# A two-block transformer kernel: two expert weight units loaded beside the ring, the context product moved behind the first expert quad

## What is computed

```python
x = x + g1 * (mix @ w_out[l])
h2 = rms_norm(x, norm2_w[l]) * (1 + sc2) + sh2
x = x + g2 * hier_moe(h2, w_group[l], b_group[l], w_expert[l], b_expert[l], w1[l], w3[l], w2[l])
...
xcn = modulate(rms_norm_2(hc, norm_mix_g[layer]), csh1, csc1)   # hc: the 256 context tokens
kv_c = xcn @ w_in[:, Q_END:]                                    # the context product
```

## Time and profile before

| what | value |
|---|---|
| median of 3 runs | 1784.64 us (1783.9 to 1785.4) |
| profiled execution, its own time | 1785.08 us |
| its span in the trace | 1783.3 us |
| PE / DVE / ACT busy | 78% / 34% / 11% |
| DMA mean | 331 GB/s |
| chain that ended last | DMA 49%, PE 43%, DVE 6% |

### The profile page before, as it was taken

One profiled execution on the slowest core, in us unless ns is written; L12 is line 12 of the kernel. 1 busy time (PEld: TensorE's weight loads), 2 busy tenths in 40 slices (PEclk: granted clock), 3 DMA queues, 4 the chain that ended last, 5 costly groups with the idle time before them and its releaser, 6 DMA issues.

```text
span 1783.3 us, 24407 instructions
## 1 busy us (share of the span) xinstructions
PE 1390.6 (78%) x10622; PEld 864.8 (48%) x10623; DVE 612.4 (34%) x968; ACT 197.6 (11%) x440; POOL 5.0 (0%) x10
## 2 busy tenths in 40 slices
PE   6798996666666756765766666667998999989997
PEld 4796863222122212221222122215876999879997
DVE  2367637000000000000000000017445777767775
ACT  2003321000000000000000000001422000120001
POOL 1000000000000000000000000000000000000000
PEclk8988998888788788788888789878998999989999
DMA  9979955999999999999999999995943555414541
GB/s 401 356 316 423 378 203 246 429 429 428 429 429 429 429 428 429 429 428 429 429 429 429 428 429 429 428 427 205 405 178 138 186 206 187 166 52 173 211 167 69
DMA packets 46263, 590.03 MB, mean 331 GB/s; under 512 B 5328, under 2 KB 7792, under 8 KB 9088
## 3 DMA queue, kind: packets, MB, share of 16 engines
q1 hardware_dynamic: 42464, 581.86, 79.0%
q10 hardware_dynamic: 3744, 7.37, 1.2%
HBM read 586.58 MB, written 2.62 MB: 330 GB/s over the span
## 4 chain that ended last, share of the span: by engine, by line
DMA 49%; PE 43%; DVE 6%; issue 1%; ACT 1%; SPq 0%; DVEq 0%; ACTq 0%
DMA ring<-in_w 44%; PE ps L1874 5%; PE ps L1875 5%; PE ps L1879 5%; PE ps L1441 3%; PE ps L1706 3%; PE ps L1613 3%; PE ps L1385 3%; PE ps L1721 2%; PE ps L1893 2%; PE ps L1892 2%; PE ps L1890 2%; DMA ring<-in_w_in 2%; DMA ring<-in_w_ada 1%; DVE ring_parts L750 1%
## 5 line engine op out<-in xcount | busy, mean ns | idle before, releaser
L1706 PE MATMUL ps<-ring,mixT 128*32 128x512 f32 x2048 | 307.1, 734 | 182.4 <-DMA ring<-in_w 180.9
L1721 PE MATMUL ps<-ring,arena 128*32 128x512 f32 x1024 | 175.3, 820 | 107.2 <-DMA ring<-in_w 96.0
L1706 PEld LDWEIGHTS ps<-ring,mixT 128*32 128x32 f32 x2048 | 62.0, 121 | 401.0 <-DMA ring<-in_w 278.0
L750 DVE TENSOR_TENSOR ring_parts<-ring,ring_parts 128x1024 fp32r<-128x1024 f32 (+3 forms) x119 | 189.7, 1625 | 1.0
L1112 DVE TENSOR_TENSOR arena<-arena,ps 128x512 f32<-128x512 f32 x16 | 11.0, 688 | 511.4 <-PE ps L1706 511.3
L1874 PE MATMUL ps<-mixT_parts,ring_parts 128*128 128x256 f32 x704 | 173.3, 283 | 6.7 <-issue 6.7
L1875 PE MATMUL ps<-mixT_parts,ring_parts 128*128 128x256 f32 x704 | 172.8, 283 | 0.0
L1721 PEld LDWEIGHTS ps<-ring,arena 128*32 128x32 f32 x1024 | 33.0, 131 | 232.8 <-DMA ring<-in_w 149.1
L747 DVE CAST ring_parts<-ring 128x1024 fp32r<-128x1024 f32 (+3 forms) x119 | 100.4, 890 | 132.4 <-DMA ring<-in_f 75.0
L1874 PEld LDWEIGHTS ps<-mixT_parts,ring_parts 128*128 128x128 f32 x704 | 134.9, 192 | 8.1 <-issue 7.2
L1875 PEld LDWEIGHTS ps<-mixT_parts,ring_parts 128*128 128x128 f32 x704 | 134.9, 192 | 0.9
(11 more groups left out here) (345 smaller groups left out, 1376.7 us busy)
## 6 DMA issues: line engine op xcount, KB each, us to landing
ring<-in_w SPq DMA_DIRECT2D x192, 2048.0 KB, 26.1
ring<-in_ada_w SPq DMA_DIRECT2D x24, 2048.0 KB, 12.5
ring<-in_f SPq DMA_DIRECT2D x22, 2048.0 KB, 8.1
ring<-in_w_ada SPq DMA_DIRECT2D x12, 2048.0 KB, 16.7
ring<-in_f SPq DMA_DIRECT2D x22, 1024.0 KB, 7.1
ring<-in_w_in SPq DMA_DIRECT2D x5, 2048.0 KB, 22.3
ring<-in_w_out SPq DMA_DIRECT2D x2, 2048.0 KB, 10.9
ring<-in_mix_in SPq DMA_DIRECT2D x2, 2048.0 KB, 16.0
```

The lines of the kernel that those rows point to most:

```text
L750: return tt(out.bitcast(F32R), v, hi, ALU.subtract)
L1706: last = mm(ps[rows[u], j, :], XeT[:, 2 * m + k, rows[u]], w[:, u, k * FE:(k + 1) * FE], start=(m == 0 and k == 0), stop=(m == 3 and k == 1))
L1721: last = mm(ps[rows[u], m, :], heT[:, k, rows[u]], w[:, u, m * 512:(m + 1) * 512], start=(k == 0), stop=(k == FE // P - 1))
```

## The change

- **Two units beside the ring.** Units 4 and 7 of quad 0 (the first and the last of w3) are loaded into `side`: arena columns 5120 to 9215, and `modrow` columns 512 to 4607. The first waits for the end of the attention (`a_done`), the second for both gate rows of block 1 (`g_ev` 1, `g_mm` 2).
- **The context product's weights** leave the ring too (`rk`, in `hT`; issued once `h2_tr` says that hT has been read). Its transposes, modulation (ACT, 8 instructions), product and copy come behind quad 0 instead of before the norm. Quad 0 is written out ahead of the loops.
- **The second gate row** (`gate_row(0, 10, 2)`) moves from behind the router's transposes to right behind `w_out`.
- **The residual** goes in column halves of 512: eight DVE instructions for four; the first column half needs only part 0 of `w_out`.
- **The overflow list** on DVE moves behind quad 0.
- **Block constants** are loaded behind the experts by SP (the tables but the pooling one, 1920 columns), and the pooling table (2048 columns, 1024 KB) in the first feed-forward layer, next to the pooling weights. Two ACT copies save block 2's gate columns of `modrow`, and the last bias is loaded after quad 0.

```diff
-            load(RK, *span(A["mix_in"], MIX_CUTS[2], MIX_CUTS[3]))
+            for n in range(UNITS):
+                src = A[("w1", "w3", "w2")[n // 4]][0:1, n % 4].rearrange("q p n -> p (q n)")
+                if n == SIDE[0]:
+                    sp.wait_ge(a_done, PAIRS)
+                    sp.dma_start(side[0], src).then_inc(side_in[0], 16)
+                elif n == SIDE[1]:
+                    sp.wait_ge(g_ev, 1)
+                    sp.wait_ge(g_mm, 2)
+                    sp.dma_start(side[1], src).then_inc(side_in[1], 16)
+                    sp.wait_ge(h2_tr, 1)
+                    sp.dma_start(rk, span(A["mix_in"], MIX_CUTS[2], MIX_CUTS[3])[0]).then_inc(context_in, 16)
+                else:
+                    load(first_unit(n), src, CHUNK)
...
-            with sp.Fori(0, E // QD) as i:
+            with sp.Fori(0, E // QD - 1) as i:
                 quad_loads(i)
...
+            for a, b in ((0, CONB["pool"][0]), (CONB["pool"][1], NCONB)):
+                sp.dma_start(conb[:, a:b], A["conb"][:, a:b]).then_inc(block2_in, 16)
             for c in range(12):
                 load(RL1 + c, A["ada_w_2"][12 + c], CHUNK)
...
                     sp.dma_start(poolw.rearrange("p k n -> p (k n)"), A["pool_w"]).then_inc(pool_in, 16)
+                    sp.dma_start(CB("pool"), A["conb"][:, CONB["pool"][0]:CONB["pool"][1]]).then_inc(pool_in, 16)
...
-            for t in range(NT):
-                if t == 0:
-                    dve.wait_ge(y_first, 1)
-                else:
-                    done(dve, RO + 1)
-                link(tt(xn[:, t, :], y[:, t, :], gB[:, :], ALU.mult))
-                tt(x[:, t, :], x[:, t, :], xn[:, t, :], ALU.add).then_inc(x_new, 1)
+            for c in range(2):
+                half = slice(c * 512, (c + 1) * 512)
+                for t in range(NT):
+                    if c == 0:
+                        done(dve, RO)
+                    elif t == 0:
+                        dve.wait_ge(y_first, 1)
+                    else:
+                        done(dve, RO + 1)
+                    link(tt(xn[:, t, half], y[:, t, half], gB[:, half], ALU.mult))
+                    last = tt(x[:, t, half], x[:, t, half], xn[:, t, half], ALU.add)
+                    if c:
+                        last.then_inc(x_new, 1)
...
+            gathered(first, 1)
+            expert_quad(first, None, slice(QD, 2 * QD), True)
+            dve.wait_ge(first.out, NT)
             link(ts(nx, cnt, float(SLOTS), None, ALU.is_gt))
...
-            pe.wait_ge(g_ev, 1)
-            pe.wait_ge(cx_n, 1)
-            for k in range(KD):
-                for t in range(NT):
-                    last = tr(...)
-            last.then_inc(cx_tr, 1)
             project_out(RO, mixT, 4, range(4), False, parts=(1,), mark=True)
...
+            gate_row(0, 10, 2)
             pe.wait_ge(x_new, NT)
             norm_tr(1, 4)
...
             gather(first, 1)
-            with pe.Fori(0, E // QD - 1) as i:
+            expert_quad(first, None, True)
+            pe.wait_ge(cx_mod, 2)
+            pe.wait_ge(first.tokT, 2)
+            for k in range(KD):
+                for t in range(NT):
+                    last = tr(...)
+            last.then_inc(cx_tr, 1)
+            w = rk.rearrange("p (k n) -> p k n", k=KD)
+            pe.wait_ge(context_in, 32)
+            pe.wait_ge(cx_T, 1)
+            for t in range(NT):
+                for k in range(KD):
+                    last = mm(ps[:, 1, t * 256:(t + 1) * 256], ctxT[:, k, t * P:(t + 1) * P], w[:, k, :], start=(k == 0),
+                              stop=(k == KD - 1))
+            last.then_inc(cx_tr, 1)
+            pe.wait_ge(cx_T, 2)
+            with pe.Fori(0, E // QD - 2) as i:
                 expert_quad(first, i, True)
```

More of the change, by code:

```diff
@@ L78 @@
 RO = RL0 + 12
-RK = RO + 2
-RE = RK + 1
-RM = RE + 3 * E
+RE = RO + 2
+RM = RE + 3 * E - 2
 RL1 = RM + 6
@@ L320, in units, with th @@
             def units(self, eng, i, n):
-                eng.wait_ge(self.used, i * UNITS + (self.before + n))
+                if i is None:
+                    aside = sum(u < n for u in SIDE)
+                    if aside:
+                        eng.wait_ge(side_used, aside)
+                    eng.wait_ge(self.used, NS + RE + n - aside)
+                else:
+                    eng.wait_ge(self.used, i * UNITS + (self.before + n))
+            def th(self, i):
+                return 1 if i is None else i + (2 if self.used is ring_used else 1)
         first, later = Signals("first"), Signals("later")
@@ L326, in build @@
         ov_used = sem("ov_used")
-        first.loaded, first.used, first.before = loaded, ring_used, NS + RE
+        first.loaded, first.used, first.before = loaded, ring_used, NS + RE + UNITS - 2
         later.loaded, later.used, later.before = ov_loaded, ov_used, NS
@@ L331, in chunk_slot, with first_unit @@
             return ring[:, n % NS, :]
+        def first_unit(n):
+            return RE + n - sum(u < n for u in SIDE)
         def done(eng, n, i=None):
@@ L614, in expert_quad @@
                 nc.scalar.activation(Ye, ps[:, 0:2, :].rearrange("p b n -> p (b n)"), ACT.Copy).then_inc(S.yc, 1)
-            with act.Fori(0, E // QD) as i:
+            expert_quad(first, None)
+            act.wait_ge(cx_tr, 1)
+            act.wait_ge(cx_mod, 1)
+            for k in range(KD):
+                last = nc.scalar.activation(ctxT[:, k, :], ps[:, k // 2, (k % 2) * T:(k % 2 + 1) * T], ACT.Identity,
+                                            scale=AcolC[:, k:k + 1], bias=BcolC[:, k:k + 1])
+            last.then_inc(cx_T, 1)
+            act.wait_ge(cx_tr, 2)
+            nc.scalar.activation(kvc.rearrange("p t n -> p (t n)"), ps[:, 1, :], ACT.Copy).then_inc(cx_T, 1)
+            act.wait_ge(side_used, 2)
+            act.dma_start(modrow[0:P:32, 3072:4608], A["adab"][2]).then_inc(bias2_in, 16)
+            with act.Fori(0, E // QD - 1) as i:
                 expert_quad(first, i)
@@ L1154, in _ @@
             nc.vector.tensor_copy(ovi, ovf).then_inc(ov_ready, 1)
-            with dve.Fori(0, E // QD - 1) as i:
+            with dve.Fori(0, E // QD - 2) as i:
                 link.enter(i, 1)
-                expert_quad(first, i, bass.ds(i * QD + QD, QD), True)
-            link.leave(E // QD - 1)
-            expert_quad(first, E // QD - 1, slice(E, E + QD), False)
+                expert_quad(first, i, bass.ds(i * QD + 2 * QD, QD), True)
+            link.leave(E // QD - 2)
+            expert_quad(first, E // QD - 2, slice(E, E + QD), False)
             dve.wait_ge(ov_ready, 1)
@@ L1690, in weights, with consumed @@
                 def weights(n):
[L1692 to L1695 removed]
+                    if i is None and n in SIDE:
+                        pe.wait_ge(side_in[SIDE.index(n)], 16)
+                        w = side[SIDE.index(n)]
+                    elif i is None:
+                        arrived(first_unit(n))
+                        w = chunk_slot(first_unit(n))
+                    elif S is first:
+                        at = RE + UNITS - 2 + n
+                        pe.wait_ge(loaded[at % NS], i * (16 * UNITS // NS) + 16 * (at // NS + 1))
+                        w = chunk_slot(at)
+                    else:
+                        pe.wait_ge(ov_loaded[(RE + n) % NS], i * (16 * QD * UNITS // NS) + 16 * QD * (n // NS + 1))
+                        w = chunk_slot(RE + n)
+                    return w.rearrange("p (u n) -> p u n", u=QD)
+                def consumed(last, n):
+                    if i is None and n in SIDE:
+                        last.then_inc(side_used, 1)
+                    else:
+                        last.then_inc(S.used, 1)
                 rows = [slice(u * SLOTS, (u + 1) * SLOTS) for u in range(QD)]
                 if S is later:
[L1699 to L1700 removed]
+                    gather(S, S.th(i))
+                pe.wait_ge(S.tokT, S.th(i))
                 for j in range(2):
```

107 lines of the change are left out of this document (49 added, 58 removed).

## The result

The changed kernel takes **1774.56 us** (median of 7 runs, 1770.67 to 1777.86) against 1785.37 (7 runs, 1783.59 to 1787.68) of the kernel before on the same chip: a ratio of 0.9941, 95% interval 0.9931 to 0.9951. Measured again in a later comparison (x9) it took 1770.44 (6 runs, 1766.26 to 1778.58) against 1785.66, ratio 0.9916 (0.9894 to 0.9939).

What follows compares the result with a forecast made beforehand. Expert-weight DMA was taken as the bound, after a stall until quad 0 starts. -9.8 - 5.6 + 2 + 2 = -11.4 from 1784.64 gave 1773.2 us; forecast range 1769.6 to 1776.6, stated range 1767.5 to 1779.5.

Steps and rivals of the forecast that it cites:

- Two units beside the ring: Expert weight stream: two units loaded in the idle stretch before quad 0 take 2 x 4.9 = 9.8 us out.
- rival D: Units aside bring nothing because one of them or the context's weights load late: 1783, no change; chance 0.04.
- The start of quad 0: Before the experts: without context work ahead of the norm and with residual halves, quad 0 starts 5.6 us earlier.
- The router product's clock: Router product before quad 0: same 2.02 us idle ahead, so 0; could give 2.4 back or cost 1.4.
- The gather's clock: First gather before quad 0: the longer gap before the ranks may halve PE's clock, costing 3.8 or 0; +2 taken.
- The break at the context product: Behind quad 0: context work delays quad 1's first slot release past 51.0 us after quad 0's start, breaking the stream; +2.
- The overflow list: DVE behind quad 0's output: the list ends before quad 1's hidden product needs DVE, with 3 us cover; 0.
- Constants and ACT copies: Late loads of tables and pooling table arrive in time, and the two ACT copies fall in waits for PE; 0.
- rival A: The clock holds: neither gather nor context product runs slow, 1769.2, or 1766.8 with a fast router product; chance 0.17.
- Rival E: Transposes do not hold the clock: router product and context's start at half clock, 1775.2; chance 0.05.
- Rival B: The stream breaks longer at the context product, 5 to 9 us instead of 2: 1776 to 1780; chance 0.15.
- Rival C: Slower than before: quad 0 and context work all at half clock, a 35 us break, 1806; chance 0.04.

Runs made afterwards that it cites:

- x9: The changed kernel itself, unedited, measured and traced a second time: 1770.44 us, ratio 0.9916 to the kernel before.
- x12: Changed kernel with context transposes inside quad 0's gather and output and the later `mix_in` cast, without unused matmuls: 1767.05 us.
- x1: Changed kernel with both side units back in the ring, the context product still behind quad 0: 1782.07 us.
- x4: Changed kernel with DVE's overflow list back ahead of quad 0's hidden product: 1783.15 us.
- x6: Kernel before with only the block constants loaded at their new, later places: 1785.49 us.
- x5: Kernel before with only the residual split in column halves: 1784.94 us.
- x2: Changed kernel with the context's transposes moved inside quad 0's gather and output: 1769.59 us.
- x10: Changed kernel with DVE's cast and its product of the 512-wide `mix_in` part moved behind the residual: 1771.13 us.
- x3: Changed kernel with the context product computed twice in a row, same result: 1780.35 us.
- x7: Changed kernel with the second gate row back behind the router's transposes: 1773.57 us.
- x8: Changed kernel with unused matmuls in PE's gaps ahead of the router product, the ranks and the gather: 1769.62 us.
- x11: Changed kernel with context transposes inside quad 0's gather and output, unused matmuls in PE's gaps, and the later `mix_in` cast: 1764.01 us.

## Why the prediction was right, and where it was not

The forecast was 1773.2, its own range 1769.6 to 1776.6 and the stated one 1767.5 to 1779.5; both measurements of the changed kernel, 1774.56 and 1770.44, lie in the narrower of them. Step by step:

- **Two units beside the ring, -9.8:** right. 9.6 us between two traces without a break, 9.7 over eleven traces. No unit aside came late; rival D falls.
- **The start of quad 0, -5.6:** right. The second half of `w_out` was in at 252.48 (DVE's release), 31.6 after the attention's end, where 251.20 - 1.74 gives 31.5. The transposes ended 36.7 after it, where the forecast had 254.4 - 218.0 = 36.4: -5.3 in place of -5.6.
- **The router product's clock, 0:** the size was off. It gave 2.5 back in the first trace, as the forecast's fast end had it (2.4), and cost 0.8 in x9 (7.05 against 6.25), where the slow end was forecast as 1.4: the product took 7.05 to 7.10 at half clock, and not the 7.6 that had been taken over from the gather's records. The premise, that the same idle of 2.02 leads to the same clock, is what failed: behind this idle the product took from 3.79 to 7.10.
- **The gather's clock, +2:** in the first trace 0 (3.81), in x9 +2.0, in x12 +2.3. The reason given, the gap before the ranks, does not decide it. That gap grew to 3.66 (3.0 was forecast) and the clock fell behind it, 0.55 in 269 to 270 and 0.50 in 270 to 272. But the ranks took the loss: the gather's idle shrank from 1.62 to 0.15, and from the ranks' start to the gather's it was 4.0 us against 3.8 before. In x9 the gap was only 2.00 and the ranks ran at full clock (0.43 for the first, as always), and yet the gather was slow.
- **The break at the context product, +2:** the mechanism was right, the size 3.0 in the first trace and 0.8 in x9. The rule of the release (51.0 after T0) held over ten traces to 0.4 us (three of them with no break to foretell), and in x1. The 3.94 us in which PE waits for ACT were forecast as 3.8. The product ran half of its time slow (0.58 in 320 to 322, 1.00 in 324 to 326) and took 8.83: half of the way between 6.9 and 13.8 was assumed, and it was a quarter. In exchange unit 11 was slow again in that trace (3.50), where full clock was assumed.
- **The overflow list, 0:** right, with more cover than worked out. It ended at 338.37, 60.5 after T0 (61 forecast), and the sum that stands behind it was due only at 347.58: 9.2 us of idle, not 3. x4 shows what its old place would have cost with the rest of the change: a wait of 10.3 us on PE and a break of 9.3. There the gain of the change is nearly gone (1783.15). That was no rival of the forecast, but it is the edit on which the two units hang.
- **Constants and ACT copies, 0:** right as far as was tried. x6 shows the constants. No run isolates the ACT copies; in the trace they take 0.40 us each at 225.8 and ACT waits 12.2 us for PE behind them.
- **What the sum left out:** the first stretch, +2.8 in this pair and nothing of the change. It hid that the two clock terms came out 4.5 us better than forecast. With the forecast's terms and the measured clock the sum is -5.3 - 2.5 - 9.6 + 3.0 = -14.4, or 1770.2, a us above rival A's 1769.2. So that the first comparison agreed with 1773.2 was in part luck: two errors stood against each other. The second measurement, 1770.44, has the size of that sum, but its trace does not show it: there T0 came only 1.4 earlier from the attention's end (63.4 against 64.8) and the cast 9.0 earlier from T0, in an execution of 1775.38.
- **The tail:** from the residual to the end it was 572.3 to 575.1 us in the eleven traces with the change in them, and 570.6 to 574.1 in the three of the kernel before, x5 and x6. Rope was never held by a constant (ACT's copy released it or it did not wait). But the means lie 1.9 apart, so a loss of a us or two behind 1210 is not excluded; no run looked for it.

**The rule on transposes.** The Trainium skill ("TensorE: Matmul & The Clock Gate", Part 4, PE-mode transpose) says of such a transpose that it doesn't count as PE-busy "the same way" and that the full clock doesn't engage for it. The earlier trace rows speaks against that, with a clock that rose over transposes alone. Rival E made of it that the router product, which has only the norm's transposes and idle ahead of it from 254.2 to 259.6, would be wholly at half clock. In the changed kernel's first trace, x1, x2 and x10 it ran at full clock (3.79 us), so rival E falls as a rule. It is not refuted as an influence: in the other traces with that idle the product did run slow, and no run puts another kind of work in the place of the transposes alone.

Rival B's band, breaks of 5 to 9 us, was reached only with added work (x3) or the list in its old place (x4). Rival C asked for all of quad 0 at half clock, and in no trace was it: its first four units together took 7.07 or 7.08 us each time.

## What to carry to other kernels

When a stream bounds the kernel and stands still ahead of that stage, each buffer that is free in the pause takes its whole transfer time out of the stream (9.6 of 9.8 us here). But it only pays while the consumer can eat what is at hand: look for the side work (here a list on DVE) that stands ahead of the first release, and compute the latest release that keeps the stream whole. That deadline, the landing of the load that takes the first freed slot less its issue-to-landing time, foretold the break or its absence in ten traces to 0.4 us; a producer on another engine between two PE steps (ACT's 3.8 us) can be put under work that PE has anyway, which took the break of 3.0 us away in x2.

## What the runs showed of the hardware

- The same instructions on PE took 57.0 to 63.7 us from the attention's end to T0 in the eight traces whose front was not edited further (the first three lines of the table), by the granted clock. Router product and gather, in us:

| kernels | router product | gather | T0 after the attention's end |
|---|---|---|---|
| changed (first trace), x2 | 3.79, 3.79 | 3.81, 3.81 | 57.0, 57.0 |
| x1, x10 | 3.79, 3.79 | 5.39, 5.43 | 58.6, 58.6 |
| x3, x4, x9 (changed again), x12 | 6.85, 6.76, 7.05, 6.78 | 6.05, 6.14, 5.85, 6.14 | 63.6, 63.7, 63.4, 63.7 |
| x7 (gate row back) | 7.10 | 3.81 | 62.0 |
| x8, x11 (unused matmuls) | 3.79, 3.79 | 3.84, 3.84 | 58.1, 56.8 |
| before, x5, x6 | 6.25, 6.64, 5.69 | 3.81, 3.81, 3.81 | 64.8, 65.2, 65.4 |

- A granted clock of 0.5 therefore did not follow from the length of the gap alone: after 2.02 us of idle the router product ran at 1.00 (260 to 264 in the changed kernel's trace) or at 0.50 (260 to 266 in x9), and after the same 3.94 us the context product ran fully at 1.00 (x3) or slow at first (changed, x9). What decides it stays open; no run here isolates it.
- The changed kernel spreads more than the one before, 7.2 and 12.3 us over its two sets of runs against 4.1 and 7.4. The stretch above accounts for 6.7 of it between traces; that it is the whole cause was not tried.
